# The second norm root moved behind the projections, four reorderings, and row projections in pairs of 512 columns

## The reference, cut to what matters

```python
h = token_mixer(rmsnorm(x, norm_mix_pre), ...);            x = x + rmsnorm(h, norm_mix_post)
h = memory_cross_attention(rmsnorm(x, norm_cross_pre), rmsnorm(mem, mem_norm), wq, wk, wv, wo)
x = x + rmsnorm(h, norm_cross_post)
h = conv_glu_ffn(rmsnorm(x, norm_ffn_pre), w_up, conv_w, conv_b, w_down); x = x + rmsnorm(h, norm_ffn_post)
x = x + hybrid_mixer(rmsnorm_2(x, norm_mix_2), w_in_2, ...)
x = x + peer_ffn(rmsnorm_2(x, norm_ffn_2), wq, subkeys, u, v)        # 16384 experts, top 16 of 8 heads
# conv_glu_ffn: gate, up = split(xn @ w_up); gate = causal_conv3(gate) + conv_b; (silu(gate) * up) @ w_down
# rmsnorm: x * rsqrt(mean(x * x) + 1e-6) * gain
```

## Time and profile before

| | |
|---|---|
| three timed runs | 1563.61, 1563.71 and 1568.01 us, median 1563.71 |
| the profiled execution | 1567.91 us, span 1566.0 us from first to last instruction |
| mean granted TensorE clock | 0.979 of full speed |
| busy | PE 95%, PEld 88%, DVE 73%, ACT 54%, POOL 1% |
| DMA | 276.41 MB, 177 GB/s over the span |

### The profile page before, as it was taken

One profiled execution on the slowest core, in us unless ns is written; L12 is line 12 of the kernel. 1 busy time (PEld: TensorE's weight loads), 2 busy tenths in 40 slices (PEclk: granted clock), 3 DMA queues, 4 the chain that ended last, 5 costly groups with the idle time before them and its releaser, 6 DMA issues.

```text
span 1566.0 us, 30024 instructions
## 1 busy us (share of the span) xinstructions
PE 1491.3 (95%) x10194; PEld 1378.2 (88%) x10194; DVE 1146.3 (73%) x2152; ACT 838.1 (54%) x1174; POOL 19.0 (1%) x25
## 2 busy tenths in 40 slices
PE   7998977999989999998999999999999999999998
PEld 6887966999869999878999999999988888889997
DVE  5767655788655566665499999999888888876665
ACT  7634555544456466654577666777633433334443
POOL 0000000000003000000000000000000000000000
PEclk9999988999999999999999999999999999999999
DMA  6452441555644532254476776444477777766553
GB/s 271 137 172 76 151 145 55 186 181 181 207 135 155 178 126 82 81 189 164 157 223 219 216 222 203 136 139 144 154 251 244 238 243 240 240 206 203 187 185 139
DMA packets 97494, 276.41 MB, mean 177 GB/s; under 512 B 10760, under 2 KB 37256, under 8 KB 96908
## 3 DMA queue, kind: packets, MB, share of 16 engines
q1 hardware_dynamic: 65664, 240.54, 47.2%
q10 hardware_dynamic: 31756, 34.88, 6.3%
HBM read 260.16 MB, written 16.26 MB: 177 GB/s over the span
## 4 chain that ended last, share of the span: by engine, by line
PE 81%; DVE 9%; ACT 5%; issue 2%; DMA 1%; PEld 0%; ACTq 0%; DVEq 0%; PEldq 0%
PE acc L1150 7%; PE acc L1154 7%; PE acc L1153 7%; PE ring L545 7%; PE ring L548 6%; PE ring L549 6%; PE acc L1072 5%; PE acc L1076 5%; PE acc L1077 5%; PE ring L1114 4%; PE acc L545 3%; PE acc L548 3%; PE acc L549 3%; DVE sb_halves L1728 3%; PE ring L1137 2%
## 5 line engine op out<-in xcount | busy, mean ns | idle before, releaser
L1728 DVE TENSOR_TENSOR sb_halves<-sb_raw,sb_halves 128x1024 fp32r<-128x1024 f32 x450 | 546.4, 1229 | 193.0 <-ACT sb_halves L1218 189.6
L1218 ACT ACTIVATE sb_halves<-sb_raw 128x1024 fp32r<-128x1024 f32 x450 | 469.7, 1058 | 316.0 <-PE acc L1150 167.3
L1072 PE MATMUL acc<-sb_XH,sb_halves 128*128 128x256 f32 x800 | 232.8, 291 | 4.6 <-ACT sb_early L1542 4.4
L545 PE MATMUL ring<-sb_XH,sb_halves 128*128 128x256 f32 x784 | 224.7, 287 | 3.1 <-DVE sb_halves L1728 3.1
L1077 PE MATMUL acc<-sb_XH,sb_halves 128*128 128x256 f32 x800 | 226.1, 283 | 0.0
L1076 PE MATMUL acc<-sb_XL,sb_halves 128*128 128x256 f32 x800 | 226.1, 283 | 0.0
L548 PE MATMUL ring<-sb_XL,sb_halves 128*128 128x256 f32 x784 | 223.5, 285 | 0.0
L549 PE MATMUL ring<-sb_XH,sb_halves 128*128 128x256 f32 x784 | 223.3, 285 | 0.0
L1150 PE MATMUL acc<-sb_halves,sb_coefh 128*128 128x512 f32 x512 | 200.3, 391 | 2.0 <-DVE sb_coefl L2278 2.0
L1153 PE MATMUL acc<-sb_halves,sb_coefh 128*128 128x512 f32 x512 | 200.0, 391 | 0.0
L1154 PE MATMUL acc<-sb_halves,sb_coefl 128*128 128x512 f32 x512 | 199.9, 390 | 0.0
(11 more groups left out here) (335 smaller groups left out, 2532.6 us busy)
## 6 DMA issues: line engine op xcount, KB each, us to landing
sb_raw<-wstream SPq DMA_DIRECT2D x450, 512.0 KB, 3.6
ahead<-sb_early ACTq DMA_DIRECT2D x100, 128.0 KB, 2.5
sb_area<-ahead ACTq DMA_DIRECT2D x98, 128.0 KB, 3.4
sb_area<-gains ACTq DMA_DIRECT2D x4, 512.0 KB, 4.4
sb_area<-consts SPq DMA_DIRECT2D x1, 1782.0 KB, 13.4
sb_area<-mem ACTq DMA_DIRECT2D x1, 1024.0 KB, 11.4
relvec<-relrow ACTq DMA_DIRECT2D x1, 1024.0 KB
sb_area<-keys ACTq DMA_DIRECT2D x1, 1024.0 KB, 5.5
```

The costliest lines, as they stand in the source:

```text
L545: ins = mm(out, w[0], x[0], start=first, stop=False)
L1072: ins = mm(o, w[0], XH[:, c, :], start=c == 0, stop=False)
L1218: A(hi[:, r, :], raw[:, r, :], ACT.Copy).then_inc(S("hi_ready"), 1)
L1728: tt(lo[:, r, :], raw[:, r, :], hi[:, r, :].bitcast(F32), ALU.subtract).then_inc(S("lo_ready"), 1)
```

## The change

**Norm.** The next projection is fed with x times the norm gain, without the root. x is transposed as it is (`tile_T`), tile 0 already between the last chunks of the output product; x is updated and signalled in halves (`x_half`), with acc signalled in halves too. `tile_XH` and `tile_XL` replace `norm_T` and `rest_norm` in pieces of 128 columns, and `proj_unscaled` replaces `proj_fresh` at the four seams (both pieces of the slot with XH first, then both with XL). The root of x is taken afterwards (`x_root`, `x_inverse`), and every consumer of a projection multiplies by it: as a column where tokens are rows, as a row (`root_T`, spread by `spread_roots`, turned by `root_row`, copied by `turned_roots`) where tokens are columns.

**Feed-forward.** The gate part and the product are each multiplied by root_T on DVE; ACT no longer copies the gate, but copies the product to hidh.

**Second mixer.** `column_scaled` on DVE replaces ACT's copies of the seven T2 projections, kc and vc.

**Experts.** The queries use buffers UH and UL; x times root is formed in xs and split into XH and XL while the queries are projected.

**Reorderings.** ACT's `feed(MEM[0])` moves ahead of the head norm's root and of the first unit's exponentials; the first cross score moves between the two halves of the second query projection; the first tile of the forgetting attention's output is transposed at the last unit but one of ATT3; the merged rows are gated, added and transposed in halves.

**Pairs.** Two 256-column slots become one product of 512 columns (`wide`): cv (2 slots), fv (2), merge (8). Their pieces are laid out to match. `merge_quarter` has 12 matmuls of 512 columns.

The diff, cut to its core:

```diff
+            def tile_T(k, t):
+                for h in range(2):
+                    b = bank(("xn", k, t, h))
+                    pe.wait_ge(S("x_half"), 4 * (k - 2) + 2 * t + h + 1)
+                    for i in range(4):
+                        c = 4 * h + i
+                        ins = nc.tensor.transpose(b[:, i * P:(i + 1) * P], x[:, t, c * P:(c + 1) * P], ident)
+                    done(ins, ("xn", k, t, h))
+            def proj_unscaled(name, key, k, X=X2):
+                banks = [bank(name)[:, 0:T], bank((*name, 1))[:, 0:T]]
+                for j in range(2):
+                    q, r = piece(key, j)
+                    for c in range(KC):
+                        if j == 0:
+                            pe.wait_ge(S("xh_chunk"), 8 * (k - 2) + c + 1)
...
+                for j in range(2):
+                    for c in range(KC):
+                        if j == 0 and c % 4 == 0:
+                            pe.wait_ge(S("xT_ready"), 4 * k + 3 + c // 4)
...
+            def root_row(k):
+                pe.wait_ge(S("root_rows"), k - 2)
+                for t in range(NT):
+                    ins = nc.tensor.transpose(acc[:, 0, 0, t * P:(t + 1) * P], root_rows[:, t, :], ident)
...
+            def wide(out, key, k, done=None, free=None, tiles=range(NT)):
+                q, r = piece((key[0], key[1] + k // 2), k % 2)
+                for t in tiles:
+                    tok = slice(t * P, (t + 1) * P)
+                    for i in range(2):
+                        c = 2 * k + i
+                        ins = mm3(out(t), (XH[:, c, tok], XL[:, c, tok]), part(r, lambda z: z[:, i * 512:(i + 1) * 512]),
+                                  c == 0, c == KC - 1, q if i == 0 and t == (tiles[0] if free is None else free) else 0)
...
-            norm_T(3)
-            proj_fresh(("up", 0), ("up", 0), 3)
-            for f in range(1, FC):
+            tile_T(3, 1)
+            proj_unscaled(("up", 0), ("up", 0), 3)
+            proj_T(("up", 1), ("up", 1))
+            root_row(3)
+            for f in range(2, FC):
                 proj_T(("up", f), ("up", f))
...
@@ ACT @@
             def acc_root(use, t):
+                for n in range(2):
+                    act.wait_ge(S("acc_ready"), 4 * (use - 1) + 2 * t + n + 1)
+                    link(A(squared[:, 0:512], acc[:, t, n, :], ACT.Square, accum_out=sbank[:, i:i + 1]), "acc_squared")
+                act.wait_ge(S("half_mean"), NT * (use - 1) + t + 1)
...
+            def tile_XH(k, g, X):
+                for t in range(NT):
+                    for h in range(2):
+                        b = got(act, ("xn", k, t, h))
+                        for i in range(4):
+                            ins = A(X[:, c, t * P:(t + 1) * P], b[:, i * P:(i + 1) * P], ACT.Copy, scale=C(g, c))
...
+            feed(MEM[0])
             for k in range(2):
                 act.wait_ge(S("hn_ms"), k + 1)
...
             joint_roots(2, ("co", 1))
+            tile_XH(3, "g_ffn", XH)
+            feed(("up", 0))
+            for t in range(NT):
+                x_root(3, t)
-            for f in range(FC + 1):
+            for f in range(1, FC + 2):
                 if f < FC:
                     feed(("up", f))
-                    b = got(act, ("up", f))
-                    link(A(gpad[:, f % 2, 2:258], b[:, 0:T], ACT.Copy), "ff_gate")
-                if f:
+                if f <= FC:
                     act.wait_ge(S("ff_conv"), f)
                     g = (f - 1) % 2
                     link(A(fa[:, g, :], fa[:, g, :], ACT.Silu), "ff_silu")
+                if f >= 2:
+                    act.wait_ge(S("ff_prod"), f - 1)
+                    link(A(hidh[:, f - 2, :], ht[:, f % 2, :], ACT.Copy), "ff_hid")
+            root_ready()
             for i in range(FC // 2 - 1):
                 feed(("down", i))
...
@@ DVE @@
             def joint(use, key):
+                    at = 4 * (use - 1) + 2 * t
+                    dve.wait_ge(S("acc_squared"), at + 1)
+                    link(tt(tmp[:, 0:512], acc[:, t, 0, :], gain[:, 0:512], ALU.mult))
+                    link(ts(half_mean[:, t:t + 1], sbank[:, 2 * t:2 * t + 1], 1.0 / DM, EPS, ALU.mult, ALU.add), "half_mean")
+                    dve.wait_ge(S("acc_squared"), at + 2)
+                    link(tt(tmp[:, 512:DM], acc[:, t, 1, :], gain[:, 512:DM], ALU.mult), "acc_free")
                     inverse(t, rms)
+                    for h in range(2):
+                        half = slice(h * 512, (h + 1) * 512)
+                        link(stt(out=x[:, t, half], in0=tmp[:, half], scalar=rstd[:, t:t + 1], in1=x[:, t, half],
+                                 op0=ALU.mult, op1=ALU.add), "x_half")
+                    remainder(2 * SLOT_AT[key] + 2 + t, (2 * SLOT_AT[key] + 2 + t) % NR)
...
+            def tile_XL(k, g, X):
+                for t in range(NT):
+                    for h in range(2):
+                        for i in range(4):
+                            ins = stt(out=X[1][:, c, tok], in0=b[:, i * P:(i + 1) * P], scalar=C(g, c),
+                                      in1=X[0][:, c, tok].bitcast(F32), op0=ALU.mult, op1=ALU.subtract)
+                        link(ins, "xT_ready")
...
+            def x_inverse():
+                for t in range(NT):
+                    dve.wait_ge(S("rms"), roots[0])
+                    ins = V.reciprocal(rstd_x[:, t:t + 1], rms_x[:, t:t + 1])
...
+            tile_XL(3, "g_ffn", (XH, XL))
+            link(V.memset(gpad[:, :, 0:2], 0.0))
+            feed(("up", 0))
+            x_inverse()
+            spread_roots()
+            feed(("up", 1))
+            turned_roots(3)
+            for f in range(1, FC + 3):
+                if 1 < f < FC:
                     feed(("up", f))
+                if f <= FC:
+                    g = f - 1
+                    link(tt(p[:, 2:258], got(dve, ("up", g))[:, 0:T], root_T, ALU.mult), "dve_step" if g else "ffn_gate")
+                    link(ts(o, p[:, 0:256], C("fconv", g), C("fb", g), ALU.mult, ALU.add))
+                    link(stt(out=o, in0=p[:, 1:257], scalar=C("fconv", 22 + g), in1=o, op0=ALU.mult, op1=ALU.add))
+                    link(stt(out=o, in0=p[:, 2:258], scalar=C("fconv", 44 + g), in1=o, op0=ALU.mult, op1=ALU.add),
                          "ff_conv")
+                if 2 <= f <= FC + 1:
+                    g = f - 2
+                    dve.wait_ge(S("ff_silu"), g + 1)
+                    link(tt(ht[:, g % 2, :], fa[:, g % 2, :], b[:, T:2 * T] if g else b[:, 0:T], ALU.mult), "ffn_up")
+                    link(tt(ht[:, g % 2, :], ht[:, g % 2, :], root_T, ALU.mult), "ff_prod")
+                if f >= 3:
+                    g = f - 3
+                    dve.wait_ge(S("ff_hid"), g + 1)
+                    link(tt(hidl[:, g, :], ht[:, g % 2, :], hidh[:, g, :].bitcast(F32), ALU.subtract), "ffn_hidden")
             for i in range(FC // 2 - 1):
                 feed(("down", i))
...
+            def column_scaled(i):
+                b = got(dve, ("T2", i)).rearrange("p (k t) -> p k t", k=2)
+                if i < 4:
+                    for e in range(2):
+                        p = slice(e * HD, (e + 1) * HD)
+                        ins = tt(foxh[p, i // 2, c:c + 2, e, :], b[p], rows(b, p), ALU.mult)
...
             def gate_branch(br, t):
+                for h in range(2):
+                    o, s = (mg[:, t, k, h * 512:(h + 1) * 512] for k in (1, 0))
+                    link(tt(o, o, acc[:, t, h, :], ALU.mult), "acc_free" if h else "dve_step")
+                    link(tt(s, s, o, ALU.add), "merged")
...
```

More of the change, by code:

```diff
@@ L933, in gated @@
                     pe.wait_ge(S("ffn_hidden"), c + 1)
-            proj_acc(3, [("down", i) for i in range(FC // 2)], (hidh, hidl), gated)
-            norm_T(4)
+            proj_acc(3, [("down", i) for i in range(FC // 2)], (hidh, hidl), gated, {(1, FC - 1): lambda: tile_T(4, 0)})
+            tile_T(4, 1)
             T2 = [("fq", 0), ("fq", 1), ("fk", 0), ("fk", 1), ("nq", 0), ("nq", 1), ("kk",)]
@@ L1420, in _ @@
             feed(("mix", 1))
+            root_ready()
             feed(("mix", 2))
             joint_roots(1, ("mix", 3))
+            tile_XH(2, "g_cross", XH)
             load_gain(1, gain)
-            norm_T(2, "g_cross")
-            for i in range(2):
-                feed(("cq", i))
-                copy_job(("cq", i), cqT[:, 2 * i:2 * i + 2, :], "cq_copied")
-            take(("co", 1), 0)
+            feed(("cq", 0))
+            for t in range(NT):
+                x_root(2, t)
+            copy_job(("cq", 0), cqT[:, 0, :], "cq_copied")
+            copy_job(("cq", 0, 1), cqT[:, 1, :], "cq_copied")
+            feed(("cq", 1))
             attention(ATT2, len(ATT1))
@@ L1447, in _ @@
             joint_roots(3, ("down", FC // 2 - 1))
-            norm_T(4, "g_mix2")
+            tile_XH(4, "g_mix2", XH)
+            for t in range(NT):
+                x_root(4, t)
```

(20 more changed lines are left out.)

463 lines of the change are left out of this document (283 added, 180 removed).

## The result

| kernel | median, us | lowest to highest | runs |
|---|---|---|---|
| before | 1564.67 | 1562.08 to 1570.37 | 19 |
| changed | 1576.88 | 1568.19 to 1581.64 | 19 |

The ratio is 1.0069, with a 95% interval of 1.0056 to 1.0081: 10.8 us slower, beyond the 0.3% that could pass for no change. The forecast was 1559.8 in a range of 1541 to 1575, with 0.20 on slower. The profiled execution took 1577.13 us.

What follows compares the result with a forecast made beforehand. PE was taken to set the end, save at seams. Seams -18.7, root rows +0.8, reorderings -12.7, pairs -3.8 and up projections +30.5 sum to -3.9 on 1567.9, carried over to a 1559.8 us median, range 1541 to 1575.

Steps and rivals of the forecast that it cites:

- The up projections: FFN up loop: ACT-DVE hand-over makes each chunk 6.82 us; with start, tail and low clock, 30.5 us lost.
- first down wait: Down product behind the up loop: its first slot starts 1.1 us late.
- third down piece: Down product: third piece stands behind the loop's tail, PE waits 7.4 us, then 2.0 more of low clock.
- The first rival: Up loop: ACT rounds ahead or hand-over is 1.1 us shorter, so PE bounds it; 1537 us, chance 0.15.
- The second: Up loop: PE's pauses bring the 1.2 GHz level; four such chunks in 20 give 1575 us, chance 0.15.
- So PE starts at +4.7 instead of +9.7: Cross seam: first projection matmul 4.7 us behind the last output matmul, once tile 1's first XH piece is there.
- The rival of small gains at the seams: Four seams: small XH and XL pieces cost as much as large, slots end 3 us later; 1572 us, chance 0.08.
- The second mixer: Stage E3 to E4, down product's end to second mixer's output product's end: forecast 12.5 us shorter.
- merging in halves: Transposed merge ahead of the second mixer's output product: takes 0.7 of a 1.55 us wait, the rest comes back.
- The fourth rival: Second mixer: DVE in the path of nine projections brings new waits of 4 to 6 us; 1564 us, chance 0.07.
- Pairs: Wide row projections: 512-column matmuls save 0.32 us a slot; 12 slots give 3.8 us.
- Memory stage and cross score: Earlier rounding of the second memory projection's pieces gains 4.0 us; earlier first cross score gains 3.0.

Runs made afterwards that it cites:

- e3_seam: Changed kernel; at four seams the second bank is requested only when reached, and tile 0's XL precedes the second piece's remainder: ratio to before 0.9990.
- e1_loop: Changed kernel with ACT's silu and copy in the up-projection loop shifted by one chunk, behind the rounding: ratio to before 0.9935.
- e5_branch: Changed kernel with DVE's remainder of the first wout 1 piece taken ahead of gate_branch(1, 1): ratio to before 1.0061.
- e11_all_mem_undone: e6_all with ACT's first feed of the memory stage put back behind the head norms' roots and first exponentials: ratio to before 0.9788.
- e6_all: Changed kernel with shifted up loop and earlier down pieces, repaired seams and earlier wout 1 remainder together: 1532.33 us, ratio to before 0.9792.
- e4_unpair: Changed kernel with 22 of 24 matmuls of each wide row projection split into two of 256 columns: ratio to before 1.0080.
- e10_all_unpair: e6_all with 22 of 24 matmuls of each wide row projection split into two of 256 columns: ratio to before 0.9822.

## Why the prediction was wrong

**The up projections: right, to a tenth of a microsecond a chunk.** Forecast was 6.82 us, measured 6.80, with eighteen waits as forecast; a first down wait of 1.1, measured 0.72; a third down piece with a wait of 7.4, measured 7.24, and low clock behind it. If the seam of the same stage is 3.6 us short of its forecast, which is what e3_seam gave back there, the FFN itself cost 27.8 us by the stage table, of 30.5; the profiles of one code differ by 1.2 in this stage. The first rival (the loop hides) is out; e1_loop shows its condition: with ACT rounding ahead of its waiting copy the same work does hide. The second (the clock falls in the loop) is out: PE's granted clock over the stretch is 1.00.

```profile
259.00:398.00 139.00, 124.36 (x1002) 121.25 (x1002) 104.60 (x175) 58.79 (x84) 0.00 (x0) 1.00 0.47 152
```

**The seams: the step that failed is "So PE starts at +4.7 instead of +9.7".** Every duration in the chain was right or better: transposes at 2.8, pieces of 128 columns at 0.27 on ACT (taken as 0.33) and 0.288 on DVE (0.32). The step listed what the projection reads and not what it writes to. The projection asks for two banks of a ring of four that the transposes hold, and DVE gives them back with XL of tile 0, behind a remainder of 1.22 us. The rows on record had a trace of it: before the change, too, the first projection matmul, with a high half, stood 0.63 us behind DVE's XL. Four seams start 2.3 us late, and e3_seam gave 12.4 us back with nothing but that mended, with starts at 4.67, 4.66, 4.65 and 2.20. The last is what the prediction named as under 2.5. The bank still sets even these starts, so the hit on 4.7 is luck. The banks are the largest part of the 13 us between forecast and measurement. The rival of small gains at the seams had the sign and a time near the measured one, but the wrong cause: the pieces were cheap.

**The second mixer, -12.5 forecast and -4.5 measured.** Of the 8.0 us missing: 3.1 are the seam; 0.8 the pairs, 20 blocks at 0.12 in place of 0.16; 1.6 a merge block of 4.43 us at a low clock; and at the output product, the forecast had merging in halves gain 0.7 of a wait of 1.55 and so left 0.85. The 1.55 went, but the piece behind it waited 2.05, with a clock of 0.66 in the 5 us that follow, 1.7 us more: 3.75, which is 2.9 against the forecast. That makes 8.4. The prediction says that the rest comes back "since the piece after is then late" and prices it at less than the wait. The queue of DVE made it more: two gate steps of 1.4 us each stand ahead of that remainder. e5_branch, which takes the remainder first, shows the low clock going and 1.46 of the wait only moving. The 2.88 us ahead of the branch product did go. The fourth rival, new waits from DVE's scaled copies, is out: no row from 484 to 600 us has a wait of 0.15 or more.

**Pairs: the term was mis-sized, 3.8 for 2.9 by the blocks or 2.4 by the stages.** The prediction took the difference of two pitches inside long runs; blocks of 12 or 24 between other work gain 0.12, not 0.16. By an estimate from the fixed cost of 2.5 ns in the Trainium skill (TensorE: Matmul & The Clock Gate, Wait — 56ns, not 53.3ns?), 288 matmuls fewer would give 0.7. Blocks and stages show more than three times that, so this figure does not describe these matmuls.

**The reorderings.** Memory stage and cross score: -4.0 and -3.0 forecast. For the score the profiles agree (2.7 to 3.4). For the memory stage the row from the start to E1 is too blunt. From the end of the memory transposes to E1 it is 65.0 us before and 61.2 in the changed kernel, -3.8 with -0.6 of pairs and +1.0 of transposes in it, so -4.2 for the reordering; e11_all_mem_undone gives 3.1. Neither is clear of noise in the timings.

Together: forecast -3.9, the seams' banks about 12, the output product's third piece 2.9, the low clock at 611 us 1.6, pairs 0.9, less 2.7 in the FFN: +10.8, against the 9.2 of the two profiles and 10.8 by the ratio. That it meets the ratio to a tenth is luck: the banks' 12 is a timed difference, good to 3 us. What the sum does show is which terms were wrong and their order of size.

## What to carry to other kernels

A step that is moved ahead needs more than its inputs: list as well the buffer that it writes, who holds it, and what stands in that engine's queue ahead of the release; here a bank given back by a computation that nobody needed yet cost four seams 2.3 us each. When two engines hand a value back and forth inside one round of a loop, let each use what the other made in the round before: the work was the same, and the chunk went from 6.80 us to the 5.76 that PE needs. And price a wait that only moves by the queue at its new place, not by what is left of the old one.

## What the runs showed of the hardware

The granted clock does not fall only behind waits. In the changed kernel it is low in a stretch where PE is busy throughout, at 611 us, and the block of 12 matmuls there takes 4.43 us for 2.83. PE's timeline, and the window around it, in which PE is busy for 10.00 of 10.00 us at a mean clock of 0.83:

```profile
611.41 0.77 PE L563 MATMUL acc<-sb_halves,sb_XH 128*128 128x512 f32 x1
...
614.91 0.39 PE L567 MATMUL acc<-sb_halves,sb_XL 128*128 128x512 f32 x1
```

```profile
606.00:616.00 10.00, 10.00 (x59) 8.43 (x58) 3.88 (x14) 7.03 (x23) 0.00 (x0) 0.83 0.31 107
```

Ahead of it stand 4.6 us of small matmuls (64, 128 and 15 columns, 606.79 to 611.41). In the changed kernel the clock falls where they end; in e3_seam it is 0.50 already in the last 1.6 us of them. The same place has a low clock in nine of the ten profiles with the wide blocks (e6_all alone has none), and in none of the three with narrow ones, two of which (e4_unpair and e10_all_unpair) have the same small matmuls ahead of the block. So part of what the pairs give may be taken back by the clock. That is not shown: no run here has the wide blocks with other work ahead of this one, which would settle it. At a second place, behind two waits of 0.99 and 1.38 us, the same code gets either clock. It is the window from 140 to 150 us, of the changed kernel and of e3_seam:

```profile
140.00:150.00 10.00, 9.43 (x82) 9.46 (x83) 9.31 (x25) 9.51 (x14) 0.00 (x0) 1.00 0.01 2
```

```profile
140.00:150.00 10.00, 10.00 (x50) 10.00 (x50) 6.71 (x20) 4.81 (x6) 0.00 (x0) 0.51 0.01 2
```

From the memory transposes to E1 the stage takes 61.2 us in five profiles of kernels with the same code there, and 66.0 or 66.1 in three, with nothing between. One such episode is worth 4.8 us, nearly half of what this change cost. It is likely a good part of why the times of one kernel spread over 8 to 13 us here. It is also why a single profile could not decide edits of 3 us unless the stage itself was compared.
